# The second MLP product as seven half-block products in place of eight, over chunks of 512 features

## What is computed

```python
def mix_and_mlp(...):
    ...
    x = x + g1 * mix
    h2 = modulate(x, norm2_w, sh2, sc2)
    return x + g2 * (jnp.square(jax.nn.relu(h2 @ w_mlp1)) @ w_mlp2)
...
    return rmsnorm(x, final_norm_w)
```

## Time and profile before

| | |
|---|---|
| time, median of 3 runs | 1266.37 us (1263.48, 1266.97, 1266.37) |
| span of the profiled execution (first to last instruction) | 1260.7 us |
| time of the profiled execution itself | not given apart from the three runs; the median is 5.7 us above the span |
| mean granted TensorE clock | 0.974 of full |
| busy: TensorE, VectorE, ScalarE, GpSimd | 1190.0, 582.9, 273.3, 521.1 us |
| matmuls, of which in the MLP | 5360, 3072 |
| HBM read, written | 83.74 MB, 4.19 MB |

### The profile page before, as it was taken

How to read it: one execution, slowest core, us unless ns; L and a number is a source line. 1 busy time by engine, 2 the same in 40 slices (tenths; PEclk the granted TensorE clock), 3 DMA queues, 4 the chain that set the end, 5 groups by cost and what they waited for, 6 DMA issues and landing times.

```text
span 1260.7 us, 13549 instructions
## 1 busy us (share of the span) xinstructions
PE 1190.0 (94%) x5360; PEld 947.6 (75%) x5360; DVE 582.9 (46%) x519; ACT 273.3 (22%) x386; POOL 521.1 (41%) x215
## 2 busy tenths in 40 slices
PE   5599999789999999989999999999999999999996
PEld 1258887567688878768888888888888888888884
DVE  3788868975842554584421133401243211244444
ACT  4145533133351322341100011100011000111112
POOL 0712233342122444445544445544455444455442
PEclk9799999789989999989999999999999999999998
DMA  9303432230101321101111111111111111111103
GB/s 377 151 34 117 134 118 86 95 120 19 33 18 34 117 112 39 49 19 66 50 49 40 45 50 50 50 50 50 49 35 49 50 50 50 50 50 50 50 18 133
DMA packets 24596, 88.45 MB, mean 70 GB/s; under 512 B 2544, under 2 KB 3824, under 8 KB 24048
## 3 DMA queue, kind: packets, MB, share of 16 engines
q1 hardware_dynamic: 24560, 87.95, 20.0%
HBM read 83.74 MB, written 4.19 MB: 70 GB/s over the span
## 4 chain that ended last, share of the span: by engine, by line
PE 84%; DVE 9%; issue 3%; DMA 1%; POOL 1%; ACT 1%; SPq 0%; DVEq 0%; POOLq 0%; ACTq 0%
PE main L563 71%; DVE tst L1291 4%; PE main L579 3%; PE main L767 1%; PE ob L595 1%; DMA xs<-xt 1%; PE sm L699 1%; PE ob L717 1%; PE sm L688 1%; PE ob L714 1%; DVE macc L1361 1%; DVE X L1573 1%; DVE qe L1381 1%; PE sm L607 1%; PE sm L724 1%
## 5 line engine op out<-in xcount | busy, mean ns | idle before, releaser
L470 POOL TENSOR_TENSOR w_hi<-raw,small 128x1024 fp32r<-128x1024 f32 x92 | 223.1, 2425 | 635.0 <-PE main L563 592.2
L563 PE MATMUL main<-a_hi,w_hi 128*128 128x512 f32 x856 | 276.0, 404 | 2.6 <-DVE a_lo L1436 2.6
L563 PE MATMUL main<-a_lo,w_hi 128*128 128x512 f32 x856 | 266.7, 393 | 0.0
L563 PE MATMUL main<-a_hi,w_lo 128*128 128x512 f32 x856 | 266.2, 392 | 0.0
L473 POOL TENSOR_TENSOR w_lo<-raw,w_hi 128x1024 fp32r<-128x1024 f32 x92 | 256.0, 2783 | 7.2
L563 PEld LDWEIGHTS main<-a_lo,w_hi 128*128 128x128 f32 x856 | 162.2, 189 | 35.1
L563 PEld LDWEIGHTS main<-a_hi,w_lo 128*128 128x128 f32 x856 | 162.1, 189 | 35.0
L563 PEld LDWEIGHTS main<-a_hi,w_hi 128*128 128x128 f32 x856 | 157.6, 190 | 39.7 <-issue 4.3
L563 PE MATMUL main<-h_hi,w_hi 128*128 128x512 f32 x480 | 149.1, 392 | 0.4 <-POOL w_lo L473 0.4
L563 PE MATMUL main<-h_lo,w_hi 128*128 128x512 f32 x480 | 149.3, 392 | 0.0
L563 PE MATMUL main<-h_hi,w_lo 128*128 128x512 f32 x480 | 148.4, 390 | 0.0
(11 more groups left out here) (226 smaller groups left out, 1115.7 us busy)
## 6 DMA issues: line engine op xcount, KB each, us to landing
raw<-wstream SPq DMA_DIRECT2D x92, 512.0 KB, 3.3
mbuf<-wm SPq DMA_DIRECT2D x32, 512.0 KB, 3.4
wmod<-wm SPq DMA_DIRECT2D x4, 2048.0 KB, 18.1
xs<-xt SPq DMA_DIRECT2D x8, 512.0 KB, 15.1
X<-xt SPq DMA_DIRECT2D x2, 2048.0 KB, 8.5
out<-X SPq DMA_DIRECT2D x16, 256.0 KB, 2.4
xs<-ct SPq DMA_DIRECT2D x1, 1024.0 KB, 10.4
small<-small_in SPq DMA_DIRECT2D x1, 320.0 KB, 21.9
```

What stands on the lines that cost most here:

```text
L470: pool.tensor_tensor(w_hi[:, b, :, :], raw[:, b, :, :], ones.unsqueeze(1).broadcast_to([P, KT, P]), ALU.mult).then_inc(linked, 1)
L563: ins = pe.matmul(main[:, bank, half * HALF:(half + 1) * HALF], w[:, slot, k, :], x[:, half * HALF:(half + 1) * HALF], start=begin, stop=end)
```

## The change

The MLP now goes over NCK = 8 chunks of 512 hidden features. The first product is as before, 4 tiles per chunk. The second product is cut into blocks of 2 x 2 x 2: hidden tiles in pairs kp (even and odd tile), output tiles in pairs (rows m = 4s + 2q + 0 and 1), tokens in halves; each 2 x 2 x 2 block product, which takes eight products of half blocks, is made with seven (one level of Strassen's scheme, in a form with four sums of each operand). For each chunk and each s of 2 there are seven products j; each has 2 q x 2 kp x 3 terms = 12 matmuls of 128x512 into one of three accumulators (A, B, C; two banks each, one per q). Some products add into an accumulator that an earlier one left (ADDS_TO), and VectorE adds the accumulator to a half block of X after each product, so 28 reads of 512 tokens per chunk.

Sums of weight quarters are made by GpSimd (`part_sums`, four per s, in float32), sums of hidden halves by VectorE (`t_made`, four per kp). High parts of weights and hidden sums are made by ScalarE (`w1_high`, `w2_high`, `t_high`), low parts by VectorE (`w1_low`, `w2_low`, `t_low`). GpSimd splits no MLP weights after the first two tiles. SP loads w2 for one s in one transfer of 1 MB. In the final norm both sums over partitions stand behind the last product, and the half of tokens 512 to 1023 comes first. The squares have a buffer per block (`sqx`); the sum of the first four is made by GpSimd.

The diff, cut (memory layout, semaphores and parts of the last norm left out):

```diff
+NCK = 2 * NFC
+NPART = 7
+ACC_A, ACC_C, ACC_B = range(3)
+PARTS = ((ACC_A, 0, 0, True), (ACC_C, 1, 1, True), (ACC_A, 0, 1, False), (ACC_C, 0, 1, False),
+         (ACC_A, 1, 1, False), (ACC_B, 0, 0, True), (ACC_A, 1, 0, False))
+ADDS_TO = {2: 0, 3: 1, 4: 2, 6: 4}
+READ_BEFORE = {3: 2, 4: 1, 5: 0}
+NPROD = 2 * NPART
...
+        def slot_of(s, j):
+            return (j + 4) % NPART if s == 0 else j
+        def operand(j):
+            return (quarter(0, 0), part_sum[:, :, :, :], quarter(0, 0), part_sum[:, :, :, :], quarter(1, 0),
+                    quarter(0, 1), quarter(1, 1))[j]
+        def product_bank(s, acc, q):
+            return bank(((2, 0, 4), (6, 4, 0))[s][acc] + q)
+        def sources(kp):
+            even, odd = hid[:, 0, :], hid[:, 1, :]
+            return (even[:, 0:HALF], t_tmp[:, 0, :], t_tmp[:, 1, :], odd[:, HALF:N], even[:, HALF:N],
+                    odd[:, 0:HALF], t_tmp[:, 0, :])
...
+            def load_chunk(c, at, odd, at_next, first=False, last=False):
+                if first:
+                    sp.wait_ge(split_done, T_MLP + 2)
+                else:
+                    sp.wait_ge(w2_lo, c * (2 * NPART))
+                load_w2(at + 8, odd)
+                if not first:
+                    sp.wait_ge(w1_lo, c * 4)
+                load_w1(at + (4 * odd + 2))
+                sp.wait_ge(w1_lo, c * 4 + 1)
+                load_w1(at + (4 * odd + 3))
+                if not last:
+                    sp.wait_ge(w1_lo, c * 4 + 2)
+                    load_w1(at_next)
+                sp.wait_ge(w2_lo, c * (2 * NPART) + NPART)
+                load_w2(at + 12, odd)
...
-            split_pairs(T_MLP // 2 + 1, NSTREAM // 2)
+            def part_sums(v, first=False):
+                pool.wait_ge(w2_loaded, v * 16 + 16)
+                if not first:
+                    pool.wait_ge(w2_lo, v * NPART + (4 - NPART))
+                ...
+                pool.tensor_tensor(held, a21, a22, ALU.add).then_inc(w2_sum, 1)
+                pool.tensor_tensor(a21, a11, a21, ALU.subtract).then_inc(w2_sum, 1)
+                pool.wait_ge(w2_sum, v * 4 + 1)
+                pool.wait_ge(w2_lo, v * NPART + 1)
+                pool.tensor_tensor(a11, held, a11, ALU.subtract).then_inc(w2_sum, 1)
+                pool.wait_ge(w2_sum, v * 4 + 3)
+                pool.wait_ge(w2_lo, v * NPART + 2)
+                pool.tensor_tensor(held, a12, a11, ALU.subtract).then_inc(w2_sum, 1)
...
+            def second_products(s, c, first):
+                v7, v14 = c * (2 * NPART) + s * NPART, c * (2 * NPROD) + s * NPROD
+                for j, (acc, _, _, begins) in enumerate(PARTS):
+                    pe.wait_ge(w2_lo, v7 + (j + 1))
+                    ...
+                    for q in range(2):
+                        if j in ADDS_TO:
+                            pe.wait_ge(x_added, v14 + (2 * ADDS_TO[j] + q + 1))
+                        for kp in range(2):
+                            if s == 0 and q == 0:
+                                pe.wait_ge(t_lo, c * (2 * NPART) + (NPART * kp + j + 1))
+                            for n, (w, x) in enumerate(((0, 0), (0, 1), (1, 0))):
+                                ins = pe.matmul(product_bank(s, acc, q), slot[:, w, q, kp, :], tset[j][:, kp, x, :],
+                                                start=begins and kp == 0 and n == 0, stop=kp == 1 and n == 2,
+                                                skip_group_check=True)
+                        ins.then_inc(prod_done, 1)
+            def chunk(c, first=False):
+                for t in range(0 if not first else 2, 4):
+                    pe.wait_ge(w1_lo, c * 4 + (t - 1))
+                    if t < 2:
+                        pe.wait_ge(x_added, c * (2 * NPROD) - (NPROD, 2)[t])
+                    else:
+                        pe.wait_ge(hid_relu, c * 6 + (1, 3)[t - 2])
+                    first_product(1 - t % 2, t % 2)
+                for s in range(2):
+                    second_products(s, c, first)
...
+            for n, half in enumerate((1, 0)):
+                cols = slice(half * HALF, (half + 1) * HALF)
+                pe.wait_ge(acc3_made, 3 * (n + 1))
+                pe.matmul(bank(2 + n), ones, acc2[:, cols], start=True, stop=False)
+                pe.wait_ge(sq3_made, 4 + 4 * (n + 1))
+                pe.matmul(bank(2 + n), ones, sqx[:, KT - 1, cols], start=False, stop=True).then_inc(sums3_done, 1)
...
+            def chunk(c, first=False, last=False):
+                one, two = slice(0, HALF), slice(HALF, N)
+                for j in range(3):
+                    ...
+                    w2_high(c, 0, j)
+                for kp in range(2):
+                    t = 2 * kp
+                    act.wait_ge(hid_done, c * 4 + (t + 1))
+                    ...
+                    hidden_part(c, 3 * kp + 1, t, slice(0, N))
+                    t_high(c, kp, 0)
+                    if kp == 0:
+                        w1_high(c * 4, 0)
+                    else:
+                        w2_high(c, 0, 3)
+                    t_high(c, kp, 1)
+                    ...
+                    hidden_part(c, 3 * kp + 2, t + 1, two)
+                    hidden_part(c, 3 * kp + 3, t + 1, one)
+                    t_high(c, kp, 2)
+                    ...
...
+            def chunk(c, first=False, last=False):
+                for j in range(3):
+                    w2_low(c, 0, j)
+                t_made(c, 0, 1, first)
+                t_low(c, 0, 0)
+                w1_low(c * 4, 0)
+                ...
+                t_made(c, 1, 2)
+                t_made(c, 1, 3)
+                t_made(c, 1, 4)
+                t_low(c, 1, 2)
+                w2_low(c, 0, 5)
+                read(c, 0, 0)
+                w2_low(c, 0, 6)
+                t_low(c, 1, 3)
+                read(c, 0, 1)
+                t_low(c, 1, 4)
+                t_low(c, 1, 5)
+                read(c, 0, 2)
+                t_low(c, 1, 6)
+                for j in range(4):
+                    read(c, 0, j + 3)
+                    w2_low(c, 1, j)
+                for j in range(4, NPART):
+                    w2_low(c, 1, j)
+                read(c, 1, 0)
+                read(c, 1, 1)
+                if not last:
+                    w1_low(c * 4 + 2, 0)
+                for j in range(2, 5 if last else 6):
+                    read(c, 1, j)
+                if not last:
+                    w1_low(c * 4 + 3, 1)
+                    read(c, 1, 6)
```

More of the change, by code:

```diff
@@ L842, in _ @@
             last_pair(KT // 2 - 1 + (M_OUT - 2) // 2 + 1, T_OUT + KT - 1, acc2_made, 0, sums2_done, mix_parts, MIX_ORDER)
-            def mlp_pair(parts, m_free, t_ready, ready=None):
-                for b in range(2):
-                    pe.wait_ge(split_done, t_ready + b)
-                    pe.wait_ge(main_free[1 - b], m_free + b)
-                    product(1 - b, b, parts, ready=ready if b == 0 else None)
             free0, ready0 = (M_MLP - 2) // 2 + 1, T_MLP + 1
@@ L887, in _, with first_product @@
-            squares_summed(acc3_made, 1, sums3_done, 1)
+                half_product(1 - b, b, of_h, 1, H_ORDER, normed).then_inc(hid_done, 1)
+            def first_product(bank_pair, slot):
+                for k in range(KT):
+                    h, l = of_h(k)
+                    for w, x, begin, end in ((w_hi, h, k == 0, False), (w_hi, l, False, False),
+                                             (w_lo, h, False, k == KT - 1)):
+                        for half in range(2):
+                            ins = pe.matmul(main[:, bank_pair, half * HALF:(half + 1) * HALF], w[:, slot, k, :],
+                                            x[:, half * HALF:(half + 1) * HALF], start=begin, stop=end)
+                ins.then_inc(hid_done, 1)
@@ new lines, in chunk @@
+            def chunk(c, first=False):
[8 more added lines that the diff above has]
+                    second_products(s, c, first)
+            chunk(0, first=True)
@@ L890, in _ @@
+            with pe.Fori(1, NCK) as c:
+                chunk(c)
+            for n, half in enumerate((1, 0)):
+                cols = slice(half * HALF, (half + 1) * HALF)
[3 more added lines that the diff above has]
+                pe.matmul(bank(2 + n), ones, sqx[:, KT - 1, cols], start=False, stop=True).then_inc(sums3_done, 1)
         @block.scalar
@@ new lines, in _, with square_out @@
+            chunk(0, first=True)
+            with act.Fori(1, NCK - 1) as c:
+                chunk(c)
+            chunk(NCK - 1, last=True)
+            def square_out(read, m, cols):
+                act.wait_ge(x_added, (NCK - 1) * 2 * NPROD + read)
+                act.activation(sqx[:, m, cols], X[:, m, cols], ACT.Square).then_inc(sq3_made, 1)
+            for m in range(4):
+                square_out(NPROD, m, slice(0, N))
+            for half, reads in ((1, (7, 8, 9, 10)), (0, (11, 12, 13, 14))):
+                for read, m in zip(reads, (4, 6, 5, 7)):
```

(33 more changed lines are left out.)

257 lines of the change are left out of this document (188 added, 69 removed).

## The result

The changed kernel takes 1232.12 us (median of 4 runs, 1228.65 to 1235.85) against 1266.65 us (4 runs, 1263.48 to 1266.97): ratio 0.9738, 95% interval 0.9712 to 0.9763. The forecast was 1231.9. What follows shows which of its terms earned that, and which only cancelled.

The account below looks back on a forecast made before the run. The prediction took TensorE's gapless matmul queue as the bound. Terms -43.5 + 2.4 + 2.5 - 1.3 + 5.4 = -34.5 gave span 1226.2; carrying 5.7 gave 1231.9 us, range 1224 to 1250.

Parts of the forecast that it names:

- The matmuls: Second product: 1536 matmuls become 1344, so 192 go at 0.2267 us each, -43.5 us.
- Rival 1: New product's matmuls step at 0.2333 us instead of 0.2267: +9.0, time 1240.9; chance 12%.
- The tight stretch: From a chunk's fourth first tile, VectorE's reads come barely in time: 0.3 us per chunk, +2.4 in all.
- Rival 2: Products 2, 3, 4 and 6 wait for late VectorE reads, from 0.1 us extra per instruction: time 1251; chance 12%.
- Rival 3: GpSimd's sums hold up VectorE's two-operand instructions in the tight work: 10 us per chunk, time 1309; chance 5%.
- The start: First MLP tiles: GpSimd's sums and weight splits delay h blocks and first ReLU; third tile at 568.6, +2.5 us.
- The ones pair: First half's sum over partitions leaves the middle of the span for behind the last matmul: -1.3 us.
- The tail: After the last matmul, both halves' normalising runs together; scalings end at 16.3, whole tail 20.1 against 14.7: +5.4 us.
- From the span to the median: The 5.7 us by which the old median stood above its profiled span, carried over to the new span.
- VectorE and the loads in one chunk: VectorE busy 45 to 52 us in 82; w2 loads about 5 us; first read of s=1 done at 23.5.

Follow-up runs that it names:

- the doubled product: Product 5 of each seven made twice, against the changed kernel; 1274.23 us, ratio 1.0084 to the kernel before.
- the early read: Read of product 0 moved one VectorE instruction earlier, before w2 low 5, against the changed kernel; 1227.30 us in one execution.
- the late read: Read of product 0 moved two VectorE instructions later, behind w2 low 6 and t low 3, against the changed kernel; 1242.70 us.
- after: The changed kernel itself, with seven products per chunk half, against the kernel before; 1232.12 us, ratio 0.9738.
- the run with two of three terms: Term w_lo*x_hi left out of the second product, splits, sums and reads kept, against the changed kernel; 1194.67 us, ratio 0.9452.
- the kernel with three edits: Changed kernel plus first chunk's weight sums after hidden tiles, product 0 read one instruction earlier, VectorE's last-norm factor in PSUM; 1221.76 us, ratio 0.9652.
- the one with the later sums: First chunk's first three weight sums, highs and lows moved behind hidden tiles 0 and 1, against the changed kernel; 1229.34 us.

## Why the prediction held

**The matmuls** (-43.5): confirmed by the doubled product, +43.5. Rival 1 (a step of 0.2333 everywhere) is out: 168 matmuls in 38.40 us are 0.2286 at most, waits counted. But the step exists. In every chunk product 2 of s=0 and the last product of s=1, the very last of the kernel too (12 steps from 1203.19 to 1205.99), go at 0.2333, and the rest at 0.2267. The prediction tied it to dense waits on h; why just these 24 of 168 have it is not shown.

**The tight stretch** (+2.4): from the third tile to the last boundary it took 679.86 before and 636.81 after, -43.1; the removed matmuls and ones pair account for -44.8, so the stretch costs +1.7, with 0.3 in a full chunk (38.40 against 168 x 0.2267 = 38.1). The instant that was said to decide, product 2 waiting for the first read, is where the six weight loads wait; its 0.16 measured 0.13 by the early read. It came in six chunks of eight, 0.8 of the 1.7. Most of the rest are the 24 matmuls per chunk that step 0.0067 slower, 0.16 per chunk, for which the prediction had no term: its 0.3 per chunk was a round number above the 0.16 that it had derived, and that it fits is luck in part. Rival 2 had the right instruction queue but no cascade behind it: the late read cost exactly what was put in front of it. Rival 3's lock exists (1.73 in place of 0.69 in the row at 688.58), but falls where VectorE has room. (The read at 541.76, which the prediction gives for reads that do not stop, has no GpSimd instruction beside it and shows nothing. The two reads at 687.26 in after do: they take 1.40 beside a sum of GpSimd, 1.41 at 680.73 with none.)

**The start** (+2.5): 3.07 in the span, 0.4 of it the landmark, so 2.7. By steps: ReLU forecast behind a high done at 563.3, measured 564.2; the third tile 569.18 for 568.6.

**The ones pair** (-1.3): taken as it was; only the sum in which it stands was tested.

**The tail** (+5.4) was the one mis-sized term: +6.9. The scalings were right, 12.9 for 13.0, and so was their end, 16.5 behind the boundary for 16.3. What failed is "From there to the end it took 1260.7 - 1256.86 = 3.8": that row was of a tail in which half of the output had left already. Before, the first store is issued at 1243.73, and while TensorE ended the last product and summed its squares the queue ran full:

```profile
1245.00:1248.00 3.00, 2.19 (x8) 1.17 (x8) 2.01 (x4) 0.63 (x1) 0.00 (x0) 1.00 1.03 382
```

With 16 stores in the tail and the last of VectorE's scalings bunched, the drain behind them took 5.15 in place of 3.8. The step should have asked what all 4.2 MB need (11 us at 380 GB/s), and how much of that the scalings leave for the end.

**From the span to the median** (+5.7) was right by accident. A profiled execution's time is 1.7 to 1.9 above its span, here and in every experiment. The rest, about 3.9, was the distance between a quick execution and the median of three, which is of the size of the landmark's spread; after, the same distance came to 2.7. The span was forecast 1.4 too low, the carry 1.2 too high, and 0.2 is what is left of both.

**VectorE and the loads in one chunk**: 47.8 us busy for 45 to 52; loads 5.1 for "about 5"; first read of s=1 at 23.3 for 23.5.

## What to carry to other kernels

Where one engine is a queue without gaps, removed instructions are worth their steps, and the work lies in showing that each read and each split is in time: walk one period against the pace of that queue, and move one read earlier and one later: the two runs tell how much slack there is (here none). When work is pulled out from under a product and into the tail, price the whole drain behind it, stores first: it has a floor that faster scalings do not move (6.2 us off them brought 3.4). A VectorE instruction that must run beside GpSimd wants one of its operands in PSUM. And once TensorE has to wait, look at the granted clock before putting the whole loss down to the wait: in the run with two of three terms the clock fell to 0.50 in six of eight chunks.

## What the runs showed that was not expected

- The spread between executions of one kernel is not spread over it: the landmark at the end of the token-mixing part moves by 6.4 us, while what follows it repeats to some 0.1 us up to the third tile. Measuring from a landmark made differences of 1 us between single executions usable. What moves in the token-mixing part stays open.
- The half products on h step at 0.2333 in the kernel before and in the kernel with three edits (565.57, 565.81, 566.04), but at 0.229 in after (564.65 to 567.40 in twelve steps) and in the one with the later sums, with the same shapes at a granted clock of 1.00. Over some 85 steps that is 0.3 to 0.4 us. It is not the code of the start: the kernel with product 5 made twice has that of after, and goes at 0.229 up to 556 and at 0.2333 from 561 on (561.19 to 563.99 in twelve steps). With three edits it lasts through the next two whole tiles, 22.40 us for 22.09. No run was made for its cause.
- Ten scalings beside GpSimd go from 12.86 to 6.67 us by the place of one operand; that GpSimd's own six then drop from 9.62 to 7.41 shows that the delay had been on both sides.
- Stores reach 377 to 382 GB/s and stay there for 9.5 us with three edits together. By that rate the 4.2 MB of this kernel's output cost 11 us, an estimate, wherever they cannot begin under the last product.
